# The conditioning and the first projection of a two-layer diffusion trunk, interleaved by quarters of the columns

## The reference

```python
    for l in range(DEPTH):
        ms = jnp.split(jax.nn.silu(c) @ ada_w[l] + ada_b[l], 6, axis=-1)      # ada_w[l]: 1024 x 6144
        mc = jnp.split(jax.nn.silu(c_ctx) @ ada_w[l] + ada_b[l], 6, axis=-1)
        h_lat = modulate(rmsnorm(x_lat, pre_mix_g[l]), ms[0], ms[1])          # h * (1 + scale) + shift
        h_ctx = modulate(rmsnorm(x_ctx, pre_mix_g[l]), mc[0], mc[1])
        p_lat = h_lat @ w_in[l]                                               # w_in[l]: 1024 x 2560
        p_ctx = h_ctx @ w_in[l]
        ...  # attention and spatial gating, output projection, residual
        ...  # SwiGLU (layer 0) or eight experts, two for each token (layer 1), residual
    return x_lat
```

## Time and profile before

| | us |
|---|---|
| median of 3 runs | 1897.06 (1896.55 to 1897.63) |
| profiled execution, device time | 1896.46 |
| profiled execution, span of the profile | 1894.7 |
| outside the span | 1.8 |
| PE busy | 1736.2 (92%) |
| DVE busy | 1420.6 (75%) |
| ACT busy | 1099.1 (58%) |

### The profile page before, as it was taken

The page is one execution under the profiler, slowest core; times in us unless marked ns, Lnnn a source line. Parts: engine busy times, 40 slices in busy tenths (PEclk is TensorE's granted clock), DMA queues, the critical chain, the costliest instruction groups (busy, mean ns, idle before and its releaser), DMA issues.

```text
span 1894.7 us, 24126 instructions
## 1 busy us (share of the span) xinstructions
PE 1736.2 (92%) x7944; PEld 1403.2 (74%) x7944; DVE 1420.6 (75%) x1663; ACT 1099.1 (58%) x1408; POOL 41.4 (2%) x73
## 2 busy tenths in 40 slices
PE   5998898999999969866899999999999999999993
PEld 2775676887878858555688888888888888888883
DVE  2755756655764585664699999999999999999994
ACT  3344445222222253444688888888888888888883
POOL 1010000000010000101000000000000000000000
PEclk8999999999999989977899999999999999999997
DMA  9737143656664515334799999999999999999992
GB/s 321 228 97 231 45 135 110 223 162 208 219 213 148 162 61 190 122 109 152 265 391 359 388 386 366 392 359 390 383 365 393 360 390 382 364 393 357 390 374 96
DMA packets 225423, 505.78 MB, mean 267 GB/s; under 512 B 16376, under 2 KB 39056, under 8 KB 225088
## 3 DMA queue, kind: packets, MB, share of 16 engines
q1 hardware_dynamic: 221120, 493.30, 72.6%
q0 software_dynamic: 4224, 11.47, 2.2%
HBM read 497.34 MB, written 19.96 MB: 273 GB/s over the span
## 4 chain that ended last, share of the span: by engine, by line
issue 53%; PE 34%; DVE 7%; ACT 3%; DMA 2%; SPq 1%; POOL 0%; POOLq 0%; ACTq 0%; DVEq 0%
PE ps L562 10%; PE ps L564 10%; PE ps L563 10%; DVE w_lo L1305 1%; DMA raw<-in_ffn_w 1%; DMA raw<-in_ada_w 1%; PE ps L756 1%; PE ps L624 1%; DVE att L1555 1%; ACT w_hi L1004 1%; DVE xs L1476 1%; DVE acc L1321 1%; DVE pr L1550 0%; DVE hT_lo L1449 0%; ACT pr L1130 0%
## 5 line engine op out<-in xcount | busy, mean ns | idle before, releaser
L1305 DVE TENSOR_TENSOR w_lo<-raw,w_hi 128x1024 fp32r<-128x1024 f32 x570 | 685.2, 1223 | 224.8 <-ACT w_hi L1004 191.1
L1217 ACT ACTIVATE w_hi<-raw 128x1024 fp32r<-128x1024 f32 x448 | 473.8, 1061 | 105.8 <-PE ps L564 105.8
L562 PE MATMUL ps<-w_hi,he_hi 128*128 128x512 f32 x896 | 354.4, 396 | 0.7 <-DVE he_lo L1704 0.7
L564 PE MATMUL ps<-w_hi,he_lo 128*128 128x512 f32 x896 | 350.0, 391 | 0.0
L563 PE MATMUL ps<-w_lo,he_hi 128*128 128x512 f32 x896 | 349.4, 390 | 0.0
L1305 DVE TENSOR_TENSOR w_lo<-raw_more,w_hi 128x1024 fp32r<-128x1024 f32 x224 | 274.0, 1225 | 45.8 <-ACT w_hi L1217 26.3
L1217 ACT ACTIVATE w_hi<-raw_more 128x1024 fp32r<-128x1024 f32 x224 | 237.8, 1063 | 53.5 <-PE ps L564 53.5
L1004 ACT ACTIVATE w_hi<-raw 128x1024 fp32r<-128x1024 f32 x122 | 128.7, 1063 | 224.5 <-PE ps L564 218.1
L564 PEld LDWEIGHTS ps<-w_hi,he_lo 128*128 128x128 f32 x896 | 168.5, 188 | 36.1
L562 PEld LDWEIGHTS ps<-w_hi,he_hi 128*128 128x128 f32 x896 | 168.7, 188 | 34.8 <-issue 1.0
L563 PEld LDWEIGHTS ps<-w_lo,he_hi 128*128 128x128 f32 x896 | 168.8, 188 | 33.9
(11 more groups left out here) (216 smaller groups left out, 1985.2 us busy)
## 6 DMA issues: line engine op xcount, KB each, us to landing
raw<-in_moe_w SPq DMA_DIRECT2D x448, 512.0 KB, 6.0
raw_more<-in_moe_w SPq DMA_DIRECT2D x224, 512.0 KB, 6.0
raw<-in_ada_w SPq DMA_DIRECT2D x96, 512.0 KB, 4.3
raw<-in_ffn_w SPq DMA_DIRECT2D x66, 512.0 KB, 4.8
raw<-in_w_in SPq DMA_DIRECT2D x40, 512.0 KB, 4.9
raw<-in_w_out SPq DMA_DIRECT2D x16, 512.0 KB, 4.8
yrows<-in_x SPq DMA_DIRECT2D x8, 512.0 KB, 8.2
xe<-xrows SPq DMA_DIRECT2D x8, 512.0 KB, 6.5
```

What stands on the lines that cost most here:

```text
L562: pe.matmul(o, lh, rh, start=start, stop=False)
L564: return pe.matmul(o, ll, rh, start=False, stop=stop)
L1217: act.activation(w_hi[:, s % SPL, :], expert_raw(i), ACT.Copy).then_inc(hi_done, 1)
L1305: dve.tensor_tensor(w_lo[:, s_ % SPL, :], src, w_hi[:, s_ % SPL, :].bitcast(F32), ALU.subtract)\
```

## The change

- The first four chunks are now quarters: quarter q is columns 256 q to 256 q + 255 of part 0 and of part 1, so each quarter gives shift and scale for two k tiles. Its 4 units have shape 128 x 4 x 256 (four k tiles by 256 columns) where a unit had 128 x 2 x 512. PE uses four matmuls of 256 columns for a unit, one for each of the four column groups of the array, where it had two of 512 columns, on two of them.
- Units are listed as quarter 0, weight unit 0, quarters 1 and 2, weight unit 1, quarter 3, weight units 2 and 3 (`QUARTERS`). The token blocks are loaded before unit 0 instead of unit 4.
- DVE does the norm of the tokens before any chunk, and for each quarter: copy, finish (three small operations), split of two k tiles of `hT`, `w_lo` of one weight unit (in quarter 0 that comes ahead of the split of `hT`).
- PE runs `project_first`: quarter 0's rows and turn, transposes of k tiles 0 and 1, quarter 1's rows, and then group 0 of the projection, with the rows and turns of the other quarters and the transposes of the following two k tiles between its matmuls. The transposes go to banks 4 and 5 in turn.
- ACT loads the table for the root ahead of the squares (a root of a constant), makes `w_hi` of weight unit 0 before `hT` of k tile 0, and of unit i after k tile 2 i + 1.

```diff
-ADA_SEQ = [(0, p, h) for p in (0, 1, 3, 4) for h in range(2)]
+ADA_SEQ = [(0, 0, q) for q in range(4)] + [(0, p, h) for p in (3, 4) for h in range(2)]
+QUARTERS = ((0,), (1, 2), (3,), ())
...
-    ada(0, 4)
+    def ada_quarter(q):
+        for part in range(2):
+            for h in range(2):
+                add(("ada", q), tall(ada_w[0], 4 * h, 4, D * part + 256 * q, 256), False, (4, 256))
...
+                if l + jn == 0:
+                    for q in QUARTERS[u]:
+                        ada_quarter(q)
                 project(j, u, u + 1)
...
+        def hT_bank(key, k):
+            return 4 + k % 2 if key == "mix0" else k
...
-                if u.k == 4:
+                if u.k == 0:
                     for b in range(NB):
                         sp.dma_start(xs[:, b, :], xv[:, b, :] if b < NLAT else cv[:, b - NLAT, :]).then_inc(s_x, 16)
...
+                    if c < 4:
+                        n = 256 * (u.a % 4 // 2)
+                        for q in range(4):
+                            m = pe.matmul(ps[32 * q:32 * q + 32, bank, n:n + 256], cstat[:, 4 * (u.a % 2) + q, :], w[:, q, :],
+                                          start=(u.a % 2 == 0), stop=(u.a % 2 == 1), tile_position=(0, 32 * q))
+                        m.then_inc(ada_used, 1)
+                        continue
...
+            def project_first():
+
+                ada_rows(0, ADA)
+                ada_turn(0, ADA)
+                turn_h("mix0", NB, (0, 1))
+                ada_rows(1, ADA)
+                for q, u in enumerate(at["in", 0, IN_ORDER[0]]):
+                    pe.wait_ge(lo_done, u.s + 1)
+                    h, lo = (view(t, u) for t in split_at(u.s))
+                    for kk in range(2):
+                        k = 2 * q + kk
+                        pe.wait_ge(sg("hT mix0"), k + 1)
+                        for b in range(NB):
+                            m = mm3(ps[:, b, :], hT_hi[:, k, P * b:P * b + P], hT_lo[:, k, P * b:P * b + P],
+                                    h[:, kk, :], lo[:, kk, :], k == 0, k == KD - 1)
+                            if k % 2 and b == NB - 1:
+                                m.then_inc(unit_used, 1)
+                            if q < 3 and kk == 0 and b == 1:
+                                ada_turn(q + 1, ADA)
+                            if q < 2 and b % 2:
+                                ada_rows(q + 2, ADA, [2 * kk + b // 2])
+                        if q < 3 and kk == 0:
+                            pe.wait_ge(sg("hT32 mix0"), 2 * q + 2)
+                            turn_h("mix0", NB, (2 * q + 2, 2 * q + 3))
...
-            for c in range(4):
-                if c == 3:
-                    turn_h("mix0", NB, range(6))
-                ada_rows(c, ADA)
-                ada_turn(c, ADA)
-            pe.wait_ge(sg("ada fin"), 4)
-            turn_h("mix0", NB, range(6, KD))
...
+            act.activation(st2[:, 127:128], cst[:, C_ONES:C_ONES + 1], ACT.Sqrt)
...
                     if key == "mix0":
-                        act.wait_ge(sg("ada fin"), 3 + k // 4)
+                        if k == 0:
+                            split_upto(first_units[key])
+                        if k % 2 == 0:
+                            act.wait_ge(sg("ada fin"), k // 2 + 1)
...
+            prenorm("mix0", NB, lambda b: None)
             for c in range(4):
-                if c == 2:
-                    prenorm("mix0", NB, lambda b: None)
-                if c == 3:
-                    split_h("mix0", range(4))
                 ada_copy(c, ADA)
                 ada_finish(c, ADA)
-            split_h("mix0", range(4, KD))
+                if c == 0:
+                    take(at["in", 0, IN_ORDER[0]][c].k + 1)
+                split_h("mix0", (2 * c, 2 * c + 1))
+                if c:
+                    take(at["in", 0, IN_ORDER[0]][c].k + 1)
```

More of the change, by code:

```diff
@@ L1048, in modulate_h @@
                     for r in range(nb // 2):
[L1049 removed]
+                        ins = act.activation(hT32[:, k, 256 * r:256 * r + 256], ps[:, hT_bank(key, k), 256 * r:256 * r + 256], ACT.Identity,
                                              bias=mod_b[:, l, which, k, r:r + 1], scale=mod_a[:, l, which, k, r:r + 1])
                     ins.then_inc(sg("hT32 " + key), 1)
[L1052 to L1058 removed]
+                    if key in first_units and k % 2:
+                        split_upto(first_units[key] + k // 2)
             def post_squares(key, half, srcs, junk_, ready):
@@ L1412, in ada_finish, with pair @@
                 new = ps[:, turn_bank(c, bank), 0:8].rearrange("p (k r) -> p k r", r=2)
+                if c < 4:
+                    def pair(i):
+                        return pcol[:, 0, i + 2 * c:i + 2 * c + 2].unsqueeze(2).to_broadcast([P, 2, 2])
+                    b, a = mod_b[:, 0, 0, 2 * c:2 * c + 2, :], mod_a[:, 0, 0, 2 * c:2 * c + 2, :]
+                    dve.tensor_tensor(b, new[:, 0:2, :], pair(0), ALU.add)
+                    link(dve.tensor_tensor(a, new[:, 2:4, :], pair(KD), ALU.add))
+                    dve.scalar_tensor_tensor(out=a, in0=a, scalar=1.0, in1=pair(48), op0=ALU.add, op1=ALU.mult).then_inc(sg("ada fin"), 1)
+                    return
                 def col(i):
@@ L1450, in split_h @@
                         .then_inc(sg("hT " + key), 1)
-                    if k % 2 and (k > 4 or key != "mix0"):
-                        split_upto(first_units[key] + (k // 2 - 2 if key == "mix0" else k // 2))
+                    if k % 2 and key != "mix0":
+                        split_upto(first_units[key] + k // 2)
             def post_gates(key, half, which, dst, srcs):
```

13 lines of the change are left out of this document (5 added, 8 removed).

## The result

The changed kernel takes 1886.17 us (median of 6 executions, 1884.41 to 1890.15) where the kernel before, timed beside it, takes 1897.35 (1895.18 to 1900.38): ratio 0.9949 [0.9937, 0.9962]. (A ratio stands with its 95% interval.) The profiled execution took 1885.67 us with a span of 1883.7, so the span is 11.0 shorter. The forecast was 1886.0, in a range of 1882.5 to 1890.5. The end is as forecast; the way there is not.

The account below looks back on a forecast made before the run. The chain of waits up to the end of the projection's group 0 bounds the kernel. Group 0 ending at 61.7 instead of 73.33 gives 11.6, less 0.6 for small waits: 11.0, so 1886.0 us beside 1897.06; range 1882.5 to 1890.5.

Parts of the forecast that it names:

- The start of the projection: Group 0's first product on PE: expected at 25.5 us instead of 49.58, after quarter 1's rows.
- Landing: Loads at the start: 1.30 to 1.33 us per 512 KB unit, quarter 1 landing at 20.9 to 24.9.
- short rows load slower: Rival, quarters' loads in 256-column pieces: 1.75 us a unit instead of 1.31, gain 7.5, time 1889.5; chance 0.08.
- The loop: Projection's PE, ACT, DVE cycle: 4.4 plus 5.75, 10.15 us a loop, 9.0 for the one with quarter 3's turn.
- my floor of PE's own work: Projection group 0: 33.4 us of PE work from 25.5, ending at 58.9 if nothing waited.
- upper price: Lone units of rows between full matmuls: 1.05 us each if changing tiling mode drains, group 0 ending at 63.5, not 61.7.
- The sum: Start and loops added up: group 0 ends at 61.7 instead of 73.33, 11.6 us sooner.
- own signs of being wrong: Products at 0.43 beyond the first few, quarter 1 landing after 25.5, PE waiting in group 1, shifts at 62 and end differing.
- The clock rival: Clock falls at the loop's last wait or thinly filled start: each 1.6 to 3.4 us, time 1887.5 to 1891; chance 0.15.
- The slow rival: Clock stays low throughout the projection's start: group 0 ends at 86.2, 12.9 late, time 1910; chance 0.03.
- DVE's lost lead: Group 0 to group 1: DVE accumulates only from 56.2, first `w_lo` ready at 58.8 before 61.7; cost nothing.
- POOL's loads: POOL's loads move later by some 5 us and are needed beyond 110 us; cost nothing.

Follow-up runs that it names:

- experiment 2: Changed kernel with all rows, turns and transposes ahead of group 0's 96 products, so no interleaving on PE; 1895.02 us, ratio 0.9991 to the kernel before.
- experiments 1 and 3: 1: kernel before with only the tokens loaded first, 1897.22 us. 3: changed kernel with tokens loaded behind quarter 0, 1894.89 us.
- warm_start: Changed kernel with nine filler matmuls on PE ahead of quarter 0's rows and behind its first three units; 1888.93 us, ratio 0.9958 to the kernel before.
- weights_ahead: Changed kernel with weight units 2 and 3 split before the two k tiles of their quarter, on ACT and DVE; 1884.50 us, ratio 0.9933 to the kernel before.
- changed_again: Changed kernel run and profiled a second time with no edit; 1887.63 us, ratio 0.9953 to the kernel before.
- long_rows: Changed kernel with the quarters' conditioning units read in rows of 512 columns, which takes the wrong columns; 1888.83 us, ratio 0.9961 to the kernel before.
- tokens_after_quarter_0: Changed kernel with the token blocks loaded ahead of unit 4, behind quarter 0, as before the change; 1894.89 us, ratio 0.9993 to the kernel before.
- warm_and_ahead: Changed kernel with both the edits of warm_start and weights_ahead; 1883.30 us, ratio 0.9935 to the kernel before.
- last_wait_filled: The kernel of warm_start with three more filler matmuls in the loop's last wait, ahead of weight unit 3's products; 1886.09 us, run once.
- warm_start_again: The kernel of warm_start run once more with no edit; 1888.14 us, run once.

## Why the prediction was right, and where it was not

**Right: what bounds it.** The chain up to group 0's end set the time. The start of the projection moved 21.4 us, group 0's end 8.5 (9.5 in the second profile), and at most 0.6 of that was lost to the end of the program. Interleaving is what pays (experiment 2: 6.9 of 8.5), and it needs the other parts to do so (experiments 1 and 3).

**The start of the projection, 25.5 forecast, 28.16 measured.** The tokens (13.0 and 13.06), the table load in their wait and the end of the norm stood as forecast. Two terms were mis-sized. *Landing*: I took 1.30 to 1.33 us for a unit from the kernel before, and 256-column rows take 1.47. The rival "short rows load slower" had the mechanism, at 1.75 a unit and a chance of 0.08. Warm_start shows its price: last of quarter 1 used at 26.32 where I had it landing at 24.9, 1.4 us. *The clock*: I took a turn at 1.05 and transposes at 1.1, and they came at 1.87 and 1.95, with the rows of quarter 1 at 0.9 a unit instead of 0.5. That costs 28.16 - 26.89 = 1.3. Together 2.7, which is the whole miss at this point.

**The loop, 36.2 forecast from the first product to group 0's end, 36.7 measured.** The structure held: transposes at 33.56, 44.20 and 53.54, so loops of 10.64 and 9.34 where I had 10.15 and 9.0; three waits for `w_lo` of 0.31, 0.32 and 1.77, where I had about 0.5, 0.5 and 1.7. Against that the first six products took 1.79 us (28.16 to 29.95), where I had 2.6 for the low clock. With these waits gone, weights_ahead needs 33.95 from first product to end, of which 0.3 is waiting; my floor of PE's own work was 33.4. That is close by compensation: the floor held 1.2 for the low clock, which weights_ahead did not pay, and too little for a lone unit of rows. From 46.62 to 47.19 such a unit takes 0.57, near the 0.6 taken, but it also delays the product on either side: from 46.29 to 47.53 there are two products and the unit, 1.24 us, of which the products explain 0.46. So between full matmuls it costs 0.78. The upper price of 1.05 is refuted even so. The Trainium skill (TensorEngine Tiling (Array Packing), Key Properties) says that a change of tiling mode drains the array; a drain may be in the 0.18 us above the 0.6 taken, but it is not the 0.45 more that the upper price had.

**The sum, right by compensation.** Forecast: 11.6 at group 0, 0.6 off for small waits, 11.0 at the end. Measured: 8.5 at group 0, 1.8 in attention, where the clock did not fall behind the 2.19, and 0.8 in small steps later. I had no term for the last two. In changed_again the same code had 9.5 at group 0 and 9.0 at the end (1885.7). So at its landmark the change is worth 8.5 to 9.5, against 11.6 forecast; that the median came out at the forecast 1886 is in part luck. Two of the prediction's own signs of being wrong came true: quarter 1 landed later than 25.5 (its last unit was used at 26.32 in warm_start, at once on landing), and the shift at group 0's end was not that at the end. By the medians and means of all executions it is worth 9.6 to 10.4, and whether what this has above 8.5 to 9.5 belongs to the change was not shown.

**The clock rival, 0.15.** Its price for the last wait was right: 8 products at 0.2 more, 1.6 us, is what experiments show (7.38 to 7.40 against 5.77 to 5.79). Its place was right too, the last wait. There it did not happen in the two profiles of the changed kernel. Its other half did: the thinly filled start, with the turn and the transposes at the low level (1.87 and 1.95, where the rival had 1.79 and 1.97). The slow rival, 1910, is refuted. The Trainium skill (TensorE: Matmul & The Clock Gate, HAM oscillation) describes work that starts throttled at every k tile; here, up to group 0's end, none of the profiles of the interleaved order showed the low level anywhere but at the start and behind the last wait. The prediction put this change on the side of that kernel, and that was a misreading: there the work was shorter than the wait behind it, here waits of 0.31 and 0.32 us stood in loops of about 10.

**Costed at nothing.** DVE's lost lead was harmless as argued: it began to accumulate at 58.96 (forecast 56.2), had group 1's first `w_lo` under way at 60.28 and ready before 64.86. POOL's loads I moved for nothing, and that was wrong in its reason: they came 10.4 us later (first issue 49.78 instead of 39.35), not 5, and now lie on top of loads of group 1 that are needed soon. ACT's timeline:

```profile
71.39 1.06 ACT L1041 ACTIVATE w_hi<-raw 128x1024 fp32r<-128x1024 f32 x1 [4.46 <-DMA raw<-in_w_in]
```

This unit was issued at 59.07 and landed 12.3 us later. Its `w_lo` was under way at 72.48 and PE needed it only at about 81 (group 1 starts near 64.7, and three units of 21.76 / 4 go ahead), so the cover of 7 us held and the cost is zero; but there was a collision, and I had seen none.

**Still open:** what decides whether the clock falls behind a wait. Behind 1.77 to 1.84 us it fell in three profiles (long_rows and both warm starts, first product at 26.70 to 26.91) and not in three (changed, changed_again, tokens_after_quarter_0, first product at 27.36 and later); behind 2.19 it fell before and in seven of the ten profiles with quarters, and not in changed, warm_and_ahead and last_wait_filled. The length of the wait alone does not decide it. Nor do these runs say why half of the executions of experiment 3 were 4 us slower.

## What to carry to other kernels

Reordering loads or splitting a stage finer pays only when the engine behind it gets the work in the new order and something fills its wait; here everything but the interleaving was worth 1.6 us, the load order alone nothing, and all together 8.5 to 9.5. Before a microsecond-sized gain is booked, compare the landmark right behind the edit with the end of the program: here the first gave 8.5 and the second 11.0, and only a second profile of the same kernel showed that most of the difference came and went with the clock. Of the waits in the loop the last, 1.77 us, was the one worth taking away, since it costs its own length and sometimes 1.6 us more; splitting the weights earlier, in four lines, gave 2.5 to 2.75 us.

## What the runs showed of the hardware that was not expected

- **The granted clock can read 1.00 where the engine is slow.** From 16 to 32 us the changed kernel's column says 1.00, and its turn takes 1.87, its transposes 1.95, and a unit of rows 1.08; later in the same profile they take 0.95, 1.09 and 0.64. With fillers ahead of them the same turn and transposes took 1.05 and 1.07 (warm_start), so it is the level of the clock. In warm_start_again the column has a fall, 0.60 from 20 to 24 us, and there the turn and the transposes stand at 1.31 and 1.95 again. At the start of these profiles the durations tell the level, and the column does not.
- **Rows of 1 KB load slower than rows of 2 KB.** From 16 to 32 us, with the queue never empty, 353 GB/s with 4836 of 5265 packets under 2 KB, against 388 with 186 of 3117. A unit of 512 KB was used every 1.47 us against 1.30 to 1.33, and long_rows, with pieces of 2 KB in the same order, brought it back to 1.33. By the Trainium skill (DMA: Bandwidth & Descriptors, Specifications) 512 bytes are enough for line rate; the runs show 353 against 388 GB/s between 1 KB and 2 KB.
- **The same wait, two outcomes.** 2.19 us behind the same instruction brought the clock down in one profile of one kernel and not in another of the same kernel, at 1.4 to 1.9 us for the stretch that follows (74.07 to 74.46 against 72.55 to 72.67). The changed kernel's executions at 1884.41 and 1890.15 have mean granted clocks of 0.968 and 0.965; as a rough estimate from these, 0.003 of 1884 us is 5.7, the size of their difference.
- **GpSimd's small loads slow large ones.** GpSimd issued 16 small loads from 49.78 to 58.30 us. From 61 to 65 us, when SyncE had units of 512 KB waiting that it had issued from 59.07 on, the queues moved:

```profile
q0 software_dynamic: 268, 0.81, 72.0%
q1 hardware_dynamic: 75, 0.17, 17.1%
```

  The columns are packets, MB and the share of the engines' time; q0 is GpSimd's queue, q1 SyncE's. Together that is 243 GB/s; from 71 to 75 us, with almost nothing but SyncE's queue, it is 399. The unit issued at 59.07 landed after 12.3 us. The same happened before, from 48 to 54 us (0.90 MB against 0.21), on loads with more time to spare. The low rates of 3 to 61 GB/s between 54 and 60 us in the changed kernel are something else: SyncE issued nothing between 49.91 and 59.07, and its queue moved 0.08 MB there.
